# Hybrid RWKV-7 / MLA decoder layer: another split of the attention output over PE's column halves, and row sums inverted after widening instead of before

## What is computed

```python
def causal_block_attention(q, k, v):           # S = 1024, 8 heads, Dq = 96, Dv = 64
    def one_block(args):                       # one block of 128 queries
        q_blk, i = args
        s = jnp.einsum('bqhd,bkhd->bhqk', q_blk, k) * scale
        s = jnp.where(kpos[None, :] <= qpos[:, None], s, -jnp.inf)
        p = jax.nn.softmax(s, axis=-1)
        return jnp.einsum('bhqk,bkhd->bqhd', p, v)
```

## Time and profile before

| | us |
|---|---|
| median of 3 runs (1351.94 to 1355.68) | 1353.78 |
| the profiled execution's own time | 1353.33 |
| its span, first to last instruction | 1351.5 |
| PE busy in the span | 1315.0 (97%) |
| DVE / ACT / POOL busy | 945.5 / 474.8 / 497.0 |
| the attention sweep of the 8 heads | about 306 to 470.9 |

### The profile page before, as it was taken

How to read it: one execution, slowest core, us unless ns; L and a number is a source line. 1 busy time by engine, 2 the same in 40 slices (tenths; PEclk the granted TensorE clock), 3 DMA queues, 4 the chain that set the end, 5 groups by cost and what they waited for, 6 DMA issues and landing times.

```text
span 1351.5 us, 23894 instructions
## 1 busy us (share of the span) xinstructions
PE 1315.0 (97%) x9900; PEld 1071.2 (79%) x9900; DVE 945.5 (70%) x1110; ACT 474.8 (35%) x796; POOL 497.0 (37%) x323
## 2 busy tenths in 40 slices
PE   7999999999999989989999999999999999999997
PEld 6877677877776789986688878888888888888886
DVE  3657975257777634439677988877777787669877
ACT  3143643146555433334104522212222444333330
POOL 0000112001876210002084778766774354444030
PEclk9999999999999999999999999999999999999999
DMA  5111444779639952224222345444436986666562
GB/s 225 62 48 32 141 157 156 184 169 292 183 101 288 221 127 53 59 64 140 87 101 94 117 137 198 142 147 164 156 125 226 356 288 219 190 198 200 190 205 106
DMA packets 147372, 214.50 MB, mean 159 GB/s; under 512 B 79960, under 2 KB 86240, under 8 KB 146624
## 3 DMA queue, kind: packets, MB, share of 16 engines
q1 hardware_dynamic: 146976, 211.92, 49.3%
q10 hardware_dynamic: 288, 1.05, 0.2%
HBM read 137.89 MB, written 66.39 MB: 151 GB/s over the span
## 4 chain that ended last, share of the span: by engine, by line
PE 49%; DVE 3%; POOL 1%; issue 1%; ACT 1%; DVEq 0%; POOLq 0%; ACTq 0%
PE banks L2523 23%; PE banks L2410 18%; PE banks L2326 5%; PE banks L2398 2%; POOL tile_h L3083 1%; PE banks L2371 1%; DVE wout_lo L2736 0%; POOL tile_s L3083 0%; DVE y_all L2756 0%; DVE first_relu L2870 0%; PE banks L2352 0%; DVE gn_scale L2747 0%; PE banks L156 0%; PE banks L2337 0%; DVE yr_full L2762 0%
## 5 line engine op out<-in xcount | busy, mean ns | idle before, releaser
L2523 PE MATMUL banks<-stage_b_hi,stage_a_hi 128*128 128x512 f32 x448 | 174.3, 389 | 0.0
L2523 PE MATMUL banks<-stage_b_lo,stage_a_hi 128*128 128x512 f32 x448 | 174.3, 389 | 0.0
L2523 PE MATMUL banks<-stage_b_hi,stage_a_lo 128*128 128x512 f32 x448 | 174.3, 389 | 0.0
L2898 DVE TENSOR_TENSOR stage_a_lo<-stage_a_raw,stage_a_hi 128x1024 fp32r<-128x1024 f32 x56 | 97.7, 1745 | 35.2 <-ACT stage_a_hi L2665 35.2
L2665 ACT ACTIVATE stage_a_hi<-stage_a_raw 128x1024 fp32r<-128x1024 f32 x56 | 59.4, 1061 | 120.9 <-DMA stage_b_raw<-in_w_ffn 98.4
L2523 PEld LDWEIGHTS banks<-stage_b_lo,stage_a_hi 128*128 128x128 f32 x448 | 84.1, 188 | 17.6
L2523 PEld LDWEIGHTS banks<-stage_b_hi,stage_a_hi 128*128 128x128 f32 x448 | 84.1, 188 | 17.4
L2523 PEld LDWEIGHTS banks<-stage_b_hi,stage_a_lo 128*128 128x128 f32 x448 | 84.1, 188 | 17.3
L852 POOL TENSOR_TENSOR hT<-hT,rate 128x1024 f32<-128x1024 f32 x4 | 13.5, 3370 | 210.1 <-DVE kk_tile L773 210.1
L428 PE MATMUL banks<-xT_hi,win_hi 128*128 128x512 f32 x288 | 90.6, 396 | 0.0
L428 PE MATMUL banks<-xT_lo,win_hi 128*128 128x512 f32 x288 | 88.8, 389 | 0.0
(11 more groups left out here) (423 smaller groups left out, 3590.1 us busy)
## 6 DMA issues: line engine op xcount, KB each, us to landing
stage_b_raw<-in_w_ffn SPq DMA_DIRECT2D x50, 512.0 KB, 5.0
stage_a_raw<-hid_s SPq DMA_DIRECT2D x32, 512.0 KB, 4.0
w_landed<-in_w_ffn SPq DMA_DIRECT2D x30, 512.0 KB, 4.7
hid_s<-tile_s SPq DMA_DIRECT2D x60, 256.0 KB, 4.4
stage_a_raw<-hid_h SPq DMA_DIRECT2D x24, 512.0 KB, 4.0
hid_h<-tile_h SPq DMA_DIRECT2D x42, 256.0 KB, 2.0
win_raw<-in_w_in SPq DMA_DIRECT2D x20, 512.0 KB, 3.6
x_tok<-in_x SPq DMA_DIRECT2D x8, 512.0 KB, 7.6
```

The lines of the kernel that those rows point to most:

```text
L2523: last = nc.tensor.matmul(ps[:, bank, :], s[a][:, j, tok], s[b][:, j, :], start=p == 0 and j == 0 and n == 0, stop=p == NP - 1 and j == 1 ...
L2898: V.tensor_tensor(s["a_lo"][:], s["a_raw"][:], s["a_hi"][:].bitcast(F32), ALU.subtract).then_inc(lo2, 1)
```

## The change

Column half 0 of a group takes query tiles 0 and 3, half 1 tiles 1 and 2 (`halves_of`). The reciprocal is taken of the sums already widened to 64 columns for each tile, 128x256 numbers in one instruction, and PE spreads it by multiplying it with the 128x128 identity, one product for each query tile. The diagonals and the small `inverse` tile go. Each group has its own wide tile, and DVE waits for the same group's last use instead of the other group's. The add of two partial sums becomes a reduction. Since half 0's two tiles no longer lie side by side, each move of a result goes in two DMAs with runs of 128 instead of 256 numbers: eight DMAs for each head instead of four.

```diff
-    inverse_diag = [mem.at(f"inverse_sums_diagonal{c}", kb, [P, 2, P]) for c, kb in enumerate((110, 190))]
+    inverse_wide = [mem.at(f"inverse_sums_wide{g}", kb, [P, 4, HD]) for g, kb in enumerate((110, 190))]
...
+    k.halves_of = ((0, 3), (1, 2))
...
                     for dst, src in ((ym_hi, k.att_hi), (ym_lo, k.att_lo)):
-                        sp.dma_start(k.quarters(dst, rows, h // 2, c).bitcast(F32),
-                                     src[64 * c:64 * c + 64, :].rearrange("p (a j) -> p a j", a=2).bitcast(F32))\
-                            .then_inc(y_moved, 16)
-            sp.wait_ge(y_moved, 64 * (NH - 1))
+                        for a in range(2):
+                            part = src[64 * c:64 * c + 64, 2 * P * a:2 * P * (a + 1)].rearrange("p (t q) -> p t q", t=2)
+                            sp.dma_start(k.quarters(dst, rows, h // 2, c)[:, a, :, :].bitcast(F32), part.bitcast(F32))\
+                                .then_inc(y_moved, 16)
+            sp.wait_ge(y_moved, 128 * (NH - 1))
...
+                    for c, (near, far) in enumerate(k.halves_of):
+                        near, far = base + near - at, base + far - at
+                        out = ps[64 * c:64 * c + 64, BANK_Y + g, 0:2 * P]
+                        if kt <= near + at:
+                            last = mm(out.rearrange("p (t q) -> p t q", t=2), v_all[:, kt, h, :],
+                                      src.rearrange("p (t q) -> p t q", q=P)[:, near:far + 1:far - near, :],
+                                      start=kt == 0, stop=False)
+                        elif kt <= far + at:
+                            last = mm(out[:, P:2 * P], v_all[:, kt, h, :], src[:, far * P:(far + 1) * P],
+                                      start=False, stop=kt == far + at)
...
-                for c in range(2):
-                    last = mm(ps[64 * c:64 * c + 64, BANK_Y + g, 2 * P:4 * P], ones[:, 0:HD],
-                              inverse_diag[c][:].rearrange("p j q -> p (j q)"), start=True, stop=True)
+                for j in range(2):
+                    for c in range(2):
+                        last = mm(ps[64 * c:64 * c + 64, BANK_Y + g, (2 + j) * P:(3 + j) * P],
+                                  inverse_wide[g][:, k.halves_of[c][j], :], ident[:], start=True, stop=True)
...
-                    step.mark(V.tensor_tensor(total[:], sums[:, 0, of], sums[:, 1, of], ALU.add))
+                    step.mark(V.reduce_sum(total[:], sums[:, :, of].rearrange("p m q -> p q m"), AX_X))
...
-                step.mark(V.reciprocal(inverse[:, of], row_sums))
-                step.wait()
-                if h or g == EARLIER:
-                    dve.wait_ge(y_done[1 - g], h + g)
-                for c in range(2):
-                    pair = inverse[:, of][:, 2 * c:2 * c + 2].rearrange("p (j o) -> p j o", o=1).to_broadcast([P, 2, P])
-                    square = ident[:].rearrange("p (o q) -> p o q", o=1).to_broadcast([P, 2, P])
-                    last = V.tensor_tensor(inverse_diag[c][:], square, pair, ALU.mult)
-                last.then_inc(inverse_ready[g], 1)
+                if h:
+                    dve.wait_ge(y_done[g], h)
+                V.reciprocal(inverse_wide[g][:], row_sums.rearrange("p (j o) -> p j o", o=1).to_broadcast([P, 4, HD]))\
+                    .then_inc(inverse_ready[g], 1)
```

More of the change, by code:

```diff
@@ L915, in mla @@
     total = mem.at("row_sums_added", 3.625, [P, 4])
-    inverse = mem.at("inverse_sums", 3.75, [P, TT])
     zeros = mem.at("zeros", 112, [P, HALF])
@@ L928, in mla @@
     halves = [slice(b * HALF, (b + 1) * HALF) for b in range(2)]
-    k.quarters = lambda x, rows, tile, c: x[rows, tile, :].rearrange("p (a c j) -> p a c j", a=2, c=2)[:, :, c, :]
+    k.halves_of = ((0, 3), (1, 2))
+    k.quarters = lambda x, rows, tile, c: x[rows, tile, :].rearrange("p (a t q) -> p a t q", a=2, t=4)\
+        [:, :, k.halves_of[c][0]:k.halves_of[c][1] + 1:k.halves_of[c][1] - k.halves_of[c][0], :]
     SOLVE_FROM = (SB - 2, 20, 15, 10, 0)
@@ L1239, in pv @@
                         pe.wait_ge(y_read[g], h)
+                base = (4, 0)[g]
                 for kt in kts:
-                    for c in range(2):
[L1242 to L1252, removed]
+                    if g == LATER:
+                        src, at = ((late_t[0][:, kt, :], 4) if kt < 4 else (late_t[1][:, kt - 4, :], 4) if kt < 6
+                                   else (late_t[2][:, kt - 6, :], 6))
+                    else:
+                        src, at = (early_t[0][:, kt, :], 0) if kt < 2 else (early_t[1][:, kt - 2, :], 2)
+                    for c, (near, far) in enumerate(k.halves_of):
[8 more added lines that the diff above has]
+                                      start=False, stop=kt == far + at)
                 if kts[-1] == (7, 3)[g]:
@@ L1534, in head_leaves @@
                 if h:
-                    pool.wait_ge(y_moved, 64 * h)
+                    pool.wait_ge(y_moved, 128 * h)
                 for g in range(2):
@@ L1941, in last_head_split @@
                     src = slice(64 * c, 64 * c + 64)
-                    wide = lambda x: x[src, :].rearrange("p (a j) -> p a j", a=2)
+                    wide = lambda x: x[src, :].rearrange("p (a t q) -> p a t q", a=2, t=2)
                     step.mark(V.tensor_copy(k.quarters(k.ym_hi, rows, tile, c), wide(k.att_out)))
```

## The result

The changed kernel takes 1358.99 us (median, 1358.24 to 1360.54) against 1352.52 us (1350.97 to 1355.68) for the kernel before in the same comparison: ratio 1.0047, 95% interval 1.0031 to 1.0063, so slower by 6.4 us. Compared again later, it gave 1.0047 (1.0033 to 1.0061). The forecast was 1355 in a range of 1348.5 to 1360. The range holds the time, 1 us from its upper end; but the loss is over 0.3%, where "the same" was given the largest chance.

What follows compares the result with a forecast made beforehand. Engines and the DMA input stream ending in `beta_all` were taken to reach the sweep's end together. Next stage's start +0.65 and half clock +0.7 sum to +1.35 us on 1353.33; against the median 1355.1, said as 1355, range 1348.5 to 1360.

Steps and rivals of the forecast that it cites:

- the same: Whole kernel: time within 0.3% (4 us), 1349.7 to 1357.8; chance 0.56.
- Later stages don't change: Stages behind attention: no change, apart from 0.7 us for half clock at the next stage's start.
- rival 2: Input stream: SP's doubled issues paid in full, heads 4 and 5 cost 5.3 us instead of 0.7; 1361 us, chance 0.20.
- PE's shorter products, DVE's reciprocal, the spread: Attention groups: products with v 0.43 us less, 256-wide reciprocal 1.75 us, spreading the inverses on PE zero change.
- Rival 3: PE: weight loads of two halves hold up short passes, nothing gained before 405, stream 2.65 us late; 1358.3 us, chance 0.10.
- "Sum ... = 3.2 us" until the stream: Attention sweep until about 405 us: engines gain 3.2 us over eight groups.
- "I take +0.7" for extra issues: Input stream: extra issues for the moves of heads 4 and 5 delay the landing of `beta_all` by 0.7 us.
- "+0.4" for short runs: Input stream: runs of 512 bytes instead of 1024 delay the landing of `beta_all` by 0.4 us.
- extra issues mostly use waiting time: SP's queue in the stream, heads 4 and 5: full queues block issues, so extra ones mostly cost nothing; bounds 0 to 2 x 2.65 us.
- The end of the stage: Attention's end: SP's head moves, started after POOL's work at 463.75, come last; next stage begins at 471.6, +0.65 us.
- Half clock ... I take +0.7: Next stage's start: first 4 us of dense matmuls may run at half clock after PE's pause; 0 to 2, taken as +0.7 us.
- Rival 1: Input stream: moves up with the engines, or DMA has slack, so the gain passes through; 1346.4 us, chance 0.17.

Runs made afterwards that it cites:

- experiment 2: The changed kernel with column halves of tiles 0,1 and 2,3 and four moves a head, as in the kernel before: 1358.09 us, ratio 1.0035.
- the last experiment: The changed kernel with six moves, ACT's wait and exps last, SP's seven loads behind head 6's moves, 36 more matmuls at PE's end: 1358.42 us, ratio 1.0031.
- part 5's kernel: The same kernel as the last experiment; its 36 added matmuls are 12 of 512 columns and 24 of 8: 1358.42 us, ratio 1.0031.

## Where the forecast held and where it failed, step by step

The terms of the forecast add up to +1.35 us; the mean of two profiles is +6.3. Of the missing 5.0, 3.2 lie in the step "Later stages don't change" and 1.8 ahead of the next stage, in the doubled moves. That the range holds 1358.99 is partly luck: it reached to 1360 for the sake of rival 2, and nearly two thirds of what was missing came from a stage that forecast and rivals held fixed.

- **PE's shorter products, DVE's reciprocal, the spread: right.** A group's last product takes 1.30 us from start to end instead of 1.74, so 0.43 less (the 1.07 of the forecast left out the array's latency). At head 7, PE starts LATER's products at 453.1 and 452.5 instead of 461.8 and 460.6: 8.4 us earlier, with 8.8 forecast (which had taken 2.7 us for a wait of 2.13). All reciprocals take 1.74 to 1.75 us, all reductions 0.15, and head 5's stall is gone (clock 1.00 in 430 to 435 instead of 0.66). In the changed kernel the reduction ended 0.4 us before POOL's two copies began, so it didn't meet them; but in the kernel of experiment 2 it did, and took no longer (timelines of POOL and DVE):

```profile
422.69 3.96 POOL L1588 COPY solved<-solve 128x1024 f32<-128x1024 f32 x2
422.69 0.15 DVE L1472 TENSOR_REDUCE row_sums_added<-row_sums 128x4 f32<-128x8 f32 x1
```

  The spread's 8 passes take 0.66 us with a latency of 0.27 in it, (0.66 - 0.27) / 7 = 0.056 apart, which is what two halves of 128-wide passes need. Rival 3 is out. The 81 ns that the Trainium skill gives (TensorE: Matmul & The Clock Gate, "Back-to-back issue gap") would make it 7 x 0.081 + 0.27 = 0.84 us; the trace doesn't agree for passes in two halves.
- **"Sum ... = 3.2 us" until the stream: nearly right.** With four moves, SP issues the first load behind head 3's moves at 403.01, before at 406.76 and 406.58: 3.7 us earlier. In the changed kernel, at 406.08 and 405.51, it is 0.9 earlier (0.5 forecast), so the doubling costs 2.8 up to there (2.65 forecast).
- **"I take +0.7" for extra issues, "+0.4" for short runs: the mis-sized term.** With the 2.65 ahead of the stream, doubling was to cost 3.75 us; it cost 5.2 at `beta_all`'s landing and 5.6 at the stage's start. Inside the stream that is 2.4 instead of 1.1. The step that failed is "extra issues mostly use waiting time". Three groups of moves added 2.6, 2.4 and 3.4 us to the queue ahead of `beta_all` (heads 3, 4 and 5, first profiles), 8.3 together and 7.8 by its issue. So SP had next to no waiting time to hide them in. Only a third was made up, and not by SP: `beta_all` landed 12.4 and 12.8 us behind its issue instead of 15.3 (with four moves). The row that led astray is the 9.0 us to landing: it is bandwidth backlog of the data ahead, and doesn't show that SP was blocked while it issued the moves. The trace of before had SP issuing head 5's four in 2.8 us (447.40 to 450.16), unblocked. As the lighter engines gave more than forecast, the landing itself came out near the forecast's 465.7: 466.8 and 465.6. Short runs as such cost nothing visible (landing 2.0 us median); cutting moves into runs of 1024 bytes cost as much.
- **The end of the stage: right in order, late in size.** The last wait is for the moves, through POOL, as forecast; they start at 465.88 and 464.54 instead of 463.75, and the stage at 473.41 and 472.06 instead of 471.6.
- **"Half clock ... I take +0.7": right in the mean**, 1.4 in one profile and 0 in the other.
- **"Later stages don't change": wrong, and half of the loss.** Of the 3.9 us in the next stage, 0.7 are the clock just named; 1.9 are the 11 trips, where PE waits more often for a block of instructions since the borders fall on other instructions. 1.3 are in the trips at the ends, which vary by up to 2.3 us from one profile of a kernel to the next, so that two profiles can't assign them.
- **Rivals.** Rival 1 is out: of PE's 8.4 us, 3.7 reached the landing with four moves, and none with eight. Rival 2 (1361) is near in time but not in mechanism: it had 5.3 us for the doubled issues of heads 4 and 5, of which 2.4 came through, and its sign, a landing past 469, didn't show. The rest of the time came from a place that no rival named.

What stays open: why, with the DMA share at 0.2, the packet of a block goes later for some places of the border than for others. That the gaps are waits for the block is read from the packets' times in every profile, and that the place matters from kernels at five places; no run changes the loading alone. The 1.3 us of the end trips are not assigned.

## What to carry to other kernels

A transfer cut in two costs its whole second issue (0.65 us here) in the queue ahead of a deadline, unless rows show the issuing engine itself blocked at that time; a long landing is no such row. Here two thirds of it reached the deadline. When the changed list of an engine is longer or shorter, every later stage of that engine is a changed stage: compare marks of later stages in at least two profiles of each kernel before calling them the same, and put the difference of a few us there beside the part that you changed. Before reordering a queue, ask what the transfer waits for besides the queue: the last experiment freed SP by 10 us, and the data was not there.

## What the runs showed of the hardware

- TensorE waits at one record in 256 for its next block of instructions. All 58 gaps over 0.26 us that the 11 trips have in 14 profiles stand there, 0.27 to 1.19 us from start to start; so do the long stalls, 1.45 to 3.86 us in the two profiles each of before and after. PE never went on earlier than 1.20 us behind the end of the block's packet.
- With weights of 128 columns, a matmul of 8 columns costs 116 ns in a row of its kind (36 in 4.18 us); with weights of 8 columns, such matmuls start 26 ns apart (24 in part 5's kernel).
- A reduction of eight sums beside POOL's copies took 0.15 us (experiment 2), an add of two operand tiles 3.56 to 3.65 (both profiles of before).
- An issue of SP takes 0.60 to 0.65 us, whether it moves 512-byte or 1024-byte runs; with the DMA engines full, single ones took 2.96 (`cum_all`) and 4.48.
- From the reciprocal of the group norm to the end of the span, 736.6 to 736.9 us pass in all 14 profiles: what scatters in this kernel's time arises ahead of it.
